# One opening stage for a two-block kernel: modulation weights streamed at the start, a table cleared inside the scan

## The reference, cut to what matters

```python
h = _layer_norm(concatenate([meta, x]), emb_ln_g, emb_ln_b)
ang = pos.astype(float32)[..., None] * inv_freq
cos, sin = cos(ang), sin(ang)
for li in range(2):
    ...                                   # attention, scan, mixture of experts -> h
# second block; x is h without the meta tokens
m_lat = (silu(c) @ w_mod + b_mod).reshape(1, 1, 6, 1024)     # w_mod: 1024 x 6144
m_ctx = (silu(c_ctx) @ w_mod + b_mod).reshape(6, 1024)
h_lat = rms_norm(x, norm_mix) * (1 + m_lat[:, :, 1]) + m_lat[:, :, 0]
h_ctx = rms_norm(ctx, norm_mix) * (1 + m_ctx[1]) + m_ctx[0]
...
```

## Time and profile before

| | us |
|---|---|
| median of three runs | 4379.66 (4377.66 to 4379.9) |
| the profiled execution | 4363.92 |
| its span | 4362.1 |
| first load of `mix_in` issued | 135.00 |
| `modulate`, first DVE instruction to the issue of `wab` | 2702.64 to 2773.67 |
| `wkv`, two times | about 295 each |

### The profile page before, as it was taken

How to read it: one execution, slowest core, us unless ns; L and a number is a source line. 1 busy time by engine, 2 the same in 40 slices (tenths; PEclk the granted TensorE clock), 3 DMA queues, 4 the chain that set the end, 5 groups by cost and what they waited for, 6 DMA issues and landing times. The chain is left out here.

```text
span 4362.1 us, 75094 instructions
## 1 busy us (share of the span) xinstructions
PE 3440.5 (79%) x32104; PEld 2327.7 (53%) x32104; DVE 1591.8 (36%) x2752; ACT 811.0 (19%) x1591; POOL 331.4 (8%) x462
## 2 busy tenths in 40 slices
PE   0698599674774897699575774777998899999998
PEld 0565499563443665599463443244765764444444
DVE  3334455512113344555421114135545651124411
ACT  0221222120221111222121221002334310010000
POOL 0000122002111000221002111000003200000000
PEclk9999699896997998799787997888999999999999
DMA  3200000014993200000016993601001022222221
GB/s 145 71 32 13 22 5 5 2 56 175 398 396 117 83 30 22 2 5 5 21 42 238 395 400 128 217 15 40 30 10 50 1 68 87 77 68 77 68 60 46
DMA packets 190336, 405.55 MB, mean 93 GB/s; under 512 B 39981, under 2 KB 139693, under 8 KB 161693
## 3 DMA queue, kind: packets, MB, share of 16 engines
q1 hardware_dynamic: 170029, 354.56, 22.4%
q0 software_dynamic: 9776, 29.92, 2.1%
q10 hardware_dynamic: 10240, 16.79, 1.1%
HBM read 384.45 MB, written 37.99 MB: 97 GB/s over the span
## 5 line engine op out<-in xcount | busy, mean ns | idle before, releaser
L2881 PE MATMUL ps<-h_lat,wt 128*128 128x512 f32 x704 | 304.2, 595 | 5.9 <-ACT h_lat L2938 5.9
L1629 PE MATMUL ps<-e_w,e_xt 128*64 128x256 f32 x2048 | 248.2, 396 | 9.2 <-DMA e_w<-in_moe_w 5.4
L588 PE MATMUL ps<-h,win 128*128 128x264 f32 x960 | 232.6, 396 | 17.4 <-DVE pad L737 15.9
L1629 PEld LDWEIGHTS ps<-e_w,e_xt 128*64 128x64 f32 x2048 | 177.7, 145 | 112.0 <-issue 64.7
L2881 PEld LDWEIGHTS ps<-h_lat,wt 128*128 128x128 f32 x704 | 134.4, 191 | 175.7 <-issue 174.4
L588 PEld LDWEIGHTS ps<-h,win 128*128 128x128 f32 x960 | 180.3, 192 | 67.9 <-issue 39.3
L1648 PE MATMUL ps<-e_w,e_hid_t 128*64 128x512 f32 x512 | 158.5, 747 | 29.3 <-ACT e_hid_t L1676 29.3
L2838 PE MATMUL ps<-h_lat,wt 128*128 128x512 f32 x384 | 168.6, 597 | 8.2 <-DMA wt<-in_w_in 8.2
L1695 DVE TENSOR_TENSOR e_hid<-ps,e_silu 64x256 f32<-64x256 f32 x64 | 38.9, 608 | 330.1 <-ACT e_silu L1670 330.1
L2899 PE MATMUL ps<-ff_up,wt 128*128 128x512 f32 x352 | 152.2, 592 | 0.0
L1210 DVE COPY_PREDICATED inv<-level,ps 112x384 f32<-112x384 int32 x176 | 103.5, 588 | 80.6 <-PE ps L1106 71.8
(11 more groups left out here) (529 smaller groups left out, 6506.6 us busy)
## 6 DMA issues: line engine op xcount, KB each, us to landing
e_w<-in_moe_w SPq DMA_DIRECT2D x192, 1024.0 KB, 10.0
wmod<-in_w_mod SPq DMA_DIRECT2D x24, 1024.0 KB, 12.9
wt<-in_w_up SPq DMA_DIRECT2D x22, 1024.0 KB, 5.1
y_rows<-e_y ACTq DMA_DIRECT2D x128, 128.0 KB, 7.4
win<-in_w_in SPq DMA_DIRECT2D x10, 1536.0 KB, 6.4
wt<-in_w_in SPq DMA_DIRECT2D x12, 1024.0 KB, 7.6
wt<-in_w_down SPq DMA_DIRECT2D x16, 704.0 KB, 4.9
wout<-in_w_out SPq DMA_DIRECT2D x8, 1024.0 KB, 5.1
```

Source lines behind the costliest of these rows:

```text
L588: last = pe.matmul(ps[:, 7, 0:HT], lhsT=ring[(s + 1) % 2][:, i, o:o + P], rhs=k.h[:, i, h * HT:(h + 1) * HT], start=(i == 0), stop=(i == K ...
L1629: last = pe.matmul(ps[half, 2 + z, 0:EH], lhsT=xt[z][:, f, :], rhs=w[:, f, :], start=(f == 0), stop=(f == KD - 1))
L2881: last = pe.matmul(o, lhsT=w[:, i, m % 2 * P:(m % 2 + 1) * P], rhs=hl[:, i, :], start=(i == 0), stop=(i == KD - 1))
```

## The change

- The four stages before the loop become one, `prelude`. SP's list: `par2`, `cst`, the seven loads of meta tokens and `x` (a semaphore for each chunk), `ident`, the first six pieces of `w_mod`, the positions, five constants, the 24 mask transfers, then the pieces 7 to 24, and waits for the masks and constants at the end.
- In `prelude` TensorE goes through the 24 pieces; behind each of the pieces 9 to 20 it makes one group of the embedding's transposes. The squares of the embedding go from DVE to ACT (with an accumulated sum), the work on a chunk begins when that chunk has landed, the blanking of the masks goes to POOL. The rotary chain follows on DVE, the sines on ACT.
- `mod` and `gain` are now made in `prelude` and kept in SBUF for the whole program.
- The clearing of `y_rows` goes to `wkv`, on SP's queue: issued at that stage's start, waited for by SP alone inside it, and done once in each of the two layers. The waits for it in the routing and in `experts` go.
- `modulate` becomes `scale_inputs`, without `w_mod`. The squares of `x` alternate between ACT and DVE, each waiting for the one before; the context's squares go from DVE to POOL. Gain is multiplied together with the reciprocal on DVE (one instruction with three inputs in place of two), and the shift is added on ACT, for `x` and then for the context.

```diff
+def prelude(k, a):
...
+            def _(sp):
+                sp.dma_start(k.par2[:, :], a["par2"]).then_inc(par_in, 16)
+                sp.dma_start(k.cst[:, :], a["k_cst"]).then_inc(par_in, 16)
+                sp.dma_start(rows[0:META, 0, :], a["meta_tokens"]).then_inc(x_in[0], 16)
...
+                for n in range(RING):
+                    stream(n)
+                sp.dma_start(pos[:, META:T], a["positions"].to_broadcast([P, SEQ])).then_inc(pos_in, 16)
...
+                sp.wait_ge(blanked, 4)
+                for half in (0, N_B):
...
+                for n in range(RING, N):
+                    stream(n)
+                sp.wait_ge(grid_in, 16 * 24)
+                sp.wait_ge(consts_in, 16 * 6)
...
+                for n in range(N):
+                    s, i = n // KD, n % KD
+                    if s == 2 and i == 0:
+                        pe.wait_ge(strip_kept, 1)
+                    pe.wait_ge(wmod_in[n % RING], 16 * (n // RING + 1))
+                    for q in range(4):
+                        last = pe.matmul(ps[32 * q:32 * q + 2, mods_of(s), :], lhsT=c[:, i, :],
+                                         rhs=ring[n % RING][:, q * 512:(q + 1) * 512],
+                                         start=(i == 0), stop=(i == KD - 1))
+                    last.then_inc(streamed, 1)
+                    if n == EMBED_AT:
+                        pe.wait_ge(consts_in, 16 * 6)
+                    if EMBED_AT <= n < EMBED_AT + 2 * NC1:
+                        turn_rows(n - EMBED_AT)
+                    if s >= 1 and i == 2:
+                        turn_strip(s - 1)
+                turn_strip(STRIPS - 1)
...
+                keep_strip(0)
+                for u in range(KD):
+                    copy_rows(u)
+                keep_strip(1)
...
 def wkv(k, a, r, key, v, kk, sig, rate, y):
...
+            @block.sync
+            def _(sp):
+                sp.dma_start(k.y_rows.rearrange("(a p) n -> a p n", p=P),
+                             a["k_zeros"][None, :, :].to_broadcast([ROWS // P, P, D])).then_inc(y_cleared, 16)
+                sp.wait_ge(y_cleared, 16)
...
+def scale_inputs(k, a, t, x, mod, gain, hl, hc):
...
+        @block.gpsimd
+        def _(gp):
+            gp.wait_ge(ctx_kept, CT)
+            for f in range(KD):
+                gp.tensor_tensor(sq_c[:, f, :], hc[:, f, :], hc[:, f, :], ALU.mult).then_inc(squared_ctx, 1)
...
+            for f in range(0, KD, 2):
+                act.activation(sq[:, f, :], x[f], ACT.Square).then_inc(squared, 1)
+                act.wait_ge(squared, f + 2)
...
+            for f in range(KD):
+                act.wait_ge(scaled, f + 1)
+                act.activation(hl[:, f, :], hl[:, f, :], ACT.Identity, bias=mod[:, f, 0:1]).then_inc(shifted, 1)
+            for f in range(KD):
+                act.wait_ge(scaled_ctx, f + 1)
+                act.activation(hc[:, f, :], hc[:, f, :], ACT.Identity, bias=mod[:, f, 1:2]).then_inc(shifted, 1)
...
             for f in range(KD):
-                dve.tensor_tensor(hl[:, f, :], x[f], st[:, :], ALU.mult).then_inc(scaled, 1)
+                dve.scalar_tensor_tensor(hl[:, f, :], x[f], gain[:, 0, f:f + 1], st[:, :], ALU.mult,
+                                         ALU.mult).then_inc(scaled, 1)
...
-        with k.stage("const_landed") as (block, landed):
-            @block.gpsimd
-            def _(gp):
-                gp.dma_start(k.y_rows.rearrange("(a p) n -> a p n", p=P),
-                             a["k_zeros"][None, :, :].to_broadcast([ROWS // P, P, D])
-                             ).then_inc(k.y_cleared, 16)
...
-        load_scan_constants(k, a)
-        embed(k, a)
-        rotary_tables(k, a)
+        prelude(k, a)
```

More of the change, by code:

```diff
@@ L290, in _ @@
                                scale=gain[:, i:i + 1]).then_inc(acts, 1)
-def embed(k, a):
+def prelude(k, a):
     nc, ps = k.nc, k.ps
[L296 to L357, removed]
@@ L389, in _ @@
                 chain = Chain(dve, steps)
-                dve.wait_ge(landed, 32)
+                dve.memset(ps[:, :, :], 0.0).then_inc(ps_clear, 1)
+                for j in range(NC1):
+                    dve.wait_ge(x_in[j], 32 if j == 0 else 16)
+                    chain(dve.tensor_reduce(st[:, 0, j:j + 1], rows[:, j, :], AX.X, ALU.add))
+                    chain(dve.tensor_scalar(st[:, 1, j:j + 1], st[:, 0, j:j + 1], 1.0 / D, None, ALU.mult))
+                    dve.tensor_scalar(rows[:, j, :], rows[:, j, :], st[:, 1, j:j + 1], None,
+                                      ALU.subtract).then_inc(centred, 1)
@@ L391, in _ @@
+                dve.wait_ge(emb_root, 1)
+                chain(dve.reciprocal(st[:, 3, :], st[:, 3, :]))
+                for j in range(NC1):
+                    dve.tensor_scalar(rows[:, j, :], rows[:, j, :], st[:, 3, j:j + 1], None,
+                                      ALU.mult).then_inc(emb_ready, 1)
+                dve.wait_ge(pos_in, 16)
+                dve.wait_ge(pos_set, 1)
                 chain(dve.tensor_copy(ang[:, :], pos[:, :]))
                 chain(dve.tensor_scalar(ang[:, :], ang[:, :], float(META), k.cst[:, 6:7], ALU.add, ALU.mult))
-                chain(dve.tensor_scalar(turn[:, :], ang[:, :], 1 / two_pi, magic, ALU.mult, ALU.add))
@@ L401, in _ @@
-                for t in (ang, turn):
-                    chain(dve.tensor_scalar(t[:, :], t[:, :], 3.1415925, -3.1415925, ALU.min, ALU.max))
[L403 to L409, removed]
+                chain(dve.tensor_scalar(half_turn[:, :], ang[:, :], 1 / two_pi, magic, ALU.mult, ALU.add))
@@ new lines, in _, with make_gain @@
+                for t in (ang, half_turn):
+                    chain(dve.tensor_scalar(t[:, :], t[:, :], 3.1415925, -3.1415925, ALU.min, ALU.max))
+                dve.nop().then_inc(ang_ready, 1)
+                b0 = COL2["b_mod"]
+                def make_gain(n, j, which, g):
+                    g0 = COL2[g]
+                    dve.scalar_tensor_tensor(k.gain[:, n, :], k.mod[:, j * KD:(j + 1) * KD, which], 1.0,
+                                             k.par2[:, g0:g0 + KD], ALU.add, ALU.mult).then_inc(gained, 1)
@@ new lines, in _ @@
+                for s in range(STRIPS):
+                    dve.wait_ge(strip_turned, s + 1)
+                    for v in range(2):
+                        last = dve.tensor_tensor(
+                            k.mod[:, s * PER:(s + 1) * PER, v].rearrange("p (q m) -> p q m", q=4),
+                            ps[:, 2:6, 8 * s:8 * s + 8].rearrange("p q (m v) -> p q m v", v=2)[:, :, :, v],
+                            k.par2[:, b0 + s * PER:b0 + (s + 1) * PER].rearrange("p (q m) -> p q m", q=4), ALU.add)
+                    last.then_inc(modded, 1)
@@ L888, in rwkv @@
         mix_out(k, a, li, y)
[L891 to L916, removed]
 def wkv(k, a, r, key, v, kk, sig, rate, y):
@@ L1771, in second_block @@
             with ExitStack() as t:
-                modulate(k, a, t, x, mod, gain, hl, hc)
+                scale_inputs(k, a, t, x, mod, gain, hl, hc)
             with ExitStack() as gl:
```

257 lines of the change are left out of this document (140 added, 117 removed).

## The result

The changed kernel took 4316.87 us (median of 4 runs, 4308.98 to 4319.5) beside 4379.78 for the kernel before (4 runs, 4377.66 to 4391.21): ratio 0.9846, 95% interval 0.9829 to 0.9862, some 63 us faster. The forecast was 4295.9 with a range of 4281 to 4318; the gain is clear of the noise, 21 us smaller than forecast, and the time lies 1.1 us inside the range's upper end. The profiled execution took 4308.98 with a span of 4307.2, 54.9 less than the one before; the sum said 83.8 less.

The account below looks back on a forecast made before the run. It took serial waits and slow transfers to bound the opening, and transfers of `w_mod` the second block's first stage; 48.9 + 34.9 = 83.8 off the span gave 4280.1, plus 15.7 to the median 4295.9, range 4281 to 4318.

Parts of the forecast that it names:

- the sum: Whole kernel: 48.9 us saved in the opening plus 34.9 in the second block's first stage, 83.8 together.
- Its own bounds, 4285 to 4298: Whole-kernel time: forecast's bounds from 5.4 + 5.1 us less to 2 us more, before the range was widened.
- a late opening: Opening: TensorE becomes its bound, or intended overlap fails; 10 us back, 4306; joint chance 0.17.
- a delayed scan: Scan stage: the clearing delays it through instruction fetch; 24 us back, 4320; chance 0.10.
- their issue itself starves nothing: Opening: mask transfers issued from about 10 to 20 us, while the first six pieces flow until about 29.
- The fourth rival: Opening: positions or masks hold up chunks, or first six pieces run dry; 10 us back, 4306; shared chance 0.17.
- The first rival: Opening: TensorE at half clock becomes the bound behind pieces 9 to 20; 10 us back, 4306; shared chance 0.17.
- the rival with 4658 us: Scan stage: clearing uses a single engine, takes 476 us and outlasts the scan; 278 us slower than before; chance 0.02.
- GpSimd's eight squares: Second block's first stage: three squares beside the reciprocal, five alternating with scalings at 0.75 + 0.79 us, from 2717.5 to 2727.6.
- The table load of 1.28 at the head: Second block's first stage: one ScalarE table load assumed for the root, 1.28 us; without it 1.3 more gain.
- Even doubled that lies within 3.5, so I take nothing: Scan stage: instruction page fetch, 1.0 us of one engine every 3.5 us, costs nothing beside the clearing.
- The second rival: Scan stage: clearing delays instruction fetch with TensorE the bound; 24 us back, 4320; chance 0.10.

## Why the prediction was right, and where it was short

**The mechanism.** Both stages were shortened as the steps have it. The stream of 24 pieces covers the embedding, the cosines end at 84.1 before the last piece, and the second block no longer waits for weights. The forecast's sign and size held. Its own bounds, 4285 to 4298, did not: the 4316.87 is inside the range only because the high end, 4318, was drawn for the rivals of a late opening and a delayed scan. Both came in part, 8.9 and 12.2 us in the profiled pair; the second block gave 5.1 more than forecast, and 12.9 us were lost elsewhere, for which the sum had no term. That these added up to 1.1 us under the high end is luck.

**The opening, 48.9 forecast, 40.0 measured.** The step that failed is "their issue itself starves nothing". It counted SP's issues at 0.43 us each with the queue full. With three to six pieces of 1 MB still to land an issue took up to 5.06 us, so piece 7 was issued at 40.21, when the six had long landed. The last piece came at 88.85 where 80.6 was forecast. Of these 8.2 us, 5.1 are the dry queue (88.85 against 83.72 once the transfers are spread), 1.6 the masks (4.6 where 3.0 was forecast), 1.5 a stream slightly slower than assumed (79.11 without masks, 77.6 by the sum). The rest is the stage's end, 0.7. The fourth rival, with its dry six pieces, named this and priced it at 10; it came true at half of that. The first rival came true only for moments: from 61.31 to 63.90 a piece and its transposes took TensorE 1.88 and 0.85 at a granted clock of 0.50, 2.59 together and over the pace, and it ran 7 us without a wait. Then the same work took 1.04 and 0.52 at the full clock, it had caught up by 68.77, and it waited for every piece after that, the last time 0.74 us at 88.85. The loads of `x` were no obstacle either: VectorE took up the first chunk at 5.95.

In the scan the clearing runs at a share of 0.70 and takes some 44 us, near the 42.8 of the earlier trace rows, so the rival with 4658 us fell. The Trainium skill, page "DMA: Bandwidth & Descriptors", section "Why a DMA increments its semaphore by 16 and not by 1", shares a transfer out by its slowest dimension, 12 engines of 16 here; the 0.70 agrees.

**The second block, 34.9 forecast, 40.0 measured.** The largest term that was too large is GpSimd's eight squares: the sum has them from 2717.5 to 2727.6, 10.1 us, and they took 5.95, which is 4.2 of the 5.1 us. A square was priced at 0.79 and starts every 0.57; a pair taking turns was priced at 1.54 and passes every 1.02; and three squares and not five lay beside the scalings. The engines do hinder each other as the prediction says: four scalings at 1.02 in place of 0.66 are 1.4 us on VectorE, and the stage is 2.3 shorter with the squares on ScalarE, where the sum had 3.8. The table load of 1.28 at the head doesn't exist, ScalarE squares at once at 2685.33; but TensorE's sums took 10.18 where 8.53 was assumed, at a mean granted clock of 0.70 against 0.83, so the squares began only 0.3 sooner. That 40.0 is the upper end of the 33 to 40 is thus chance.

By the rule of the Trainium skill, page "SBUF — State Buffer", section "SBUF: two separate sides", by which the two exclude each other for whole instructions, a pair would take 0.57 + 0.66 = 1.23 us, an estimate from the steps of each engine alone. The measured 1.02 with alternating starts agrees with taking turns, and is 0.2 shorter than whole instructions one after the other.

**The clearing, nothing forecast, 12.2 lost in the profiled pair, 13.4 by the table's means (2 x 6.7).** The step that failed is "Even doubled that lies within 3.5, so I take nothing": it reckoned an instruction page at 1.0 us whatever the queues hold. The second rival came true at half its price of 24. The transfers of the same window, changed kernel and before:

```profile
q1 hardware_dynamic: 203, 12.58, 69.1%
q8 instruction: 7, 0.11, 1.0%
```

```profile
q8 instruction: 7, 0.11, 1.0%
q14 instruction: 1, 0.01, 0.1%
```

As many instruction pages come, and their packets take as long, 1.0% of 16 engines; a page doesn't get slower once an engine serves it. But the clearing's 203 packets share 69.1% of 16 engines' 44 us, so each holds its engine for 2.4 us. The transfers around the hole from 509.3 to 512.42 show when its page came, first from 507 to 510.00, then from 510.00 to 510.20:

```profile
q1 hardware_dynamic: 13, 0.85, 66.9%
```

```profile
q1 hardware_dynamic: 2, 0.13, 186.8%
q8 instruction: 1, 0.02, 28.8%
```

No page starts in the 3 us before 510.00; one starts just behind it, when TensorE has stood for 0.8 us, and TensorE goes on 2.3 us after the page's start. So it is with all 23 holes of 1.5 us or more that the scans of the seven kernels with a clearing there have: each ends 2.1 to 2.8 us after the start of a page, and a scan has only one page in 4 us. The small holes of 0.4 us and more in the scans without a clearing end so too, 2.2 to 3.0 us after a page's start, but for one of 0.5 near each scan's end. The holes are late instruction pages. That the clearing makes them late, and only in the scan, is shown by place and dose. That a page waits behind the clearing's packets on its engine is argued: the 2.4 us of a packet fit the holes of 2 to 4, but the profile doesn't say when a page was asked for.

With two clearings the holes grow from 20.0 (mean of the kernels without) to 45.2 us over both scans, 25.2 of the 45.8 that the scans grow. The rest is TensorE's lower clock, as its busy time shows for the same 9680 matmuls of a scan (kernel before, layers 1 and 2; then cleared twice; the column behind the busy time is the clock):

```profile
521.78:819.86 298.08, 271.30 (x9680) 0.98 0.02 4
1805.25:2108.72 303.47, 272.37 (x9680) 0.98 0.02 4
```

```profile
483.20:806.05 322.85, 282.76 (x9680) 0.93 0.20 82
1796.88:2120.33 323.45, 283.17 (x9680) 0.93 0.20 82
```

TensorE works 22.3 us longer, at a mean clock of 0.93 in place of 0.98. With one clearing it is 274.9 and 274.7, at 0.97: 3.6 and 2.4 us more, about half of what the changed kernel's two scans lost. The Trainium skill, page "Runtime: NRT & Kernel Launch", section "Instruction fetch mechanics", calls the crossing of a page mostly hidden; that agrees with the scans without a clearing, whose holes are under 1 us, and not with those beside the clearing.

**Elsewhere, 12.9 lost, none forecast.** The largest piece that could be placed is the boundary before layer 2's `mix_in`. Timeline of the kernel before and of the changed one, from the layer norm's last shifts:

```profile
1409.05 5.86 ACT L289 ACTIVATE h<-h,par 128x528 f32<-128x528 f32 x8 [4.26 <-DVE h L277]
1416.47 0.39 SPq L540 DMA_DIRECT2D win<-in_w_in  x1
```

```profile
1380.84 5.85 ACT L289 ACTIVATE h<-h,par 128x528 f32<-128x528 f32 x8 [4.26 <-DVE h L277]
...
1391.47 0.40 SPq L649 DMA_DIRECT2D win<-in_w_in  x1
```

From the start of the shifts to the load it is 7.42 before and 10.63 after, 3.2 us more. It is 10.2 to 11.6 in every variant, the kernel before with its clearing moved among them, and also where the clearing doesn't run in the scan. So it goes with the changed programs of the engines and not with traffic. The transfers point at instruction pages here too: in the 9 us before the load the kernel before has none at all, and the changed kernel has six instruction packets, starting 2.6 to 3.4 us before the load; every variant has six or more in its 9 us. No experiment moved them, so this stays a reading of transfers.

The rest isn't placed. Against the kernel before, the changed one loses 8.9 us between layer 1's scan and that load (the 3.2 among them), 5.6 behind layer 2's scan and 2.3 behind the load of `wab`, and its two `mix_in` are 3.9 shorter. From the end of layer 1's scan to that load the one profile of the kernel before has 596.6 us and the nine others 602.6 to 607.7, the kernel with its clearing alone moved 602.9; behind layer 2's scan it is 593.8 against 594.9 to 604.3. Two profiles of the changed kernel differ by 2.9 and 4.5 there, and the profiled execution of the kernel before was 15.7 under its median. So part of the 12.9 belongs to the change and part may be that execution's luck; one profile of the kernel before can't tell.

**Profile and median.** The distance between the profiled execution and the median was 7.9 after, not the 15.7 that the forecast kept; that is why the median was missed by 21 and the profile by 29.

## What to carry to other kernels

An issuing engine is a queue too: before small transfers are put behind a deep prefetch, look at how long an issue takes while large transfers are on their way, and put the next large piece ahead of them or spread them between the pieces. A bulk copy that needs no compute engine is still not free beside a stretch of many small unrolled instructions; put it beside large matmuls, look for idle time put to "issue", and hold the ends of the holes against the starts of the instruction packets. A mean over a group of instructions can hide two regimes: look at the shortest and the longest before saying how two engines share. Read a change of some microseconds in its own stage, over several profiles, since two executions of this kernel differed by 11 us.

## What was not expected of the hardware

- An issue on SP that took 0.43 us on a quiet queue took up to 5.06 us with three to six transfers of 1 MB still to land.
- 24 mask transfers of at most 54 KB cost all DMA engines 4.6 us inside a saturated stream, 0.19 us each.
- A copy of 12.6 MB beside the scan's small matmuls opened holes of 2.0 to 4.0 us in TensorE's stream, each ending 2.1 to 2.8 us after the start of an instruction page, and cost a scan 6.7 us on the mean, and 16.2 more for a second; beside attention it cost nothing that can be told.
- GpSimd's squares and VectorE's scalings took turns, a pair every 1.02 us; alone they start every 0.57 and 0.66 us.
